# Last block of a two-block network: where the delta rule's key products, first inverses, solve and chunks stand in the hand-written order

## The chip, the cores and the metric

The kernel runs on one core of one Trainium2 chip. The metric is the time of one execution on the device, in microseconds (us), as the median of several runs. A core has a matrix engine (TensorE, PE in the profile; its weight loads are PEld), a vector engine (DVE), an activation engine (ACT), GpSimd (POOL) and a queue that issues the large loads (SP). Each engine runs its own program in order and waits for the others on counters.

## What is computed

The reference is a network of two parts on 512 tokens of width 1024. The first part is two layers with four mixers and a mixture of 16 experts. The second part, the last block, is what the change touches. Cut to what matters here:

```python
def second_block(x, ...):
    h = rmsnorm(x, ln1[l]);  proj = h @ w_in[l]
    qkv_a, z_a, b_a, a_a, q_b, k_b, v_b = jnp.split(proj, IN_SPLITS, axis=-1)
    y_a = gated_deltanet(qkv_a, z_a, b_a, a_a, ...)      # 4 heads of 128
    y_b = dilated_attention(q_b, k_b, v_b, slopes)       # 8 heads of 64
    x = x + concatenate([y_a, y_b]) @ w_out[l]
    ...                                                  # then a gated FFN of width 2816

def chunk_gated_delta_rule(q, k, v, g, beta):            # within gated_deltanet
    decay = exp(where(causal, g_i - g_j, -inf))
    a = where(strict, (k * beta) @ k.T * decay, 0)       # per chunk
    u, w = solve((I + a), [v * beta, k * beta * exp(g)])
    a_qk = where(causal, q @ k.T * decay, 0)
    for each chunk:                                      # a recurrence over the state
        v_new = u - w @ state
        o = (q * exp(g)) @ state + a_qk @ v_new
        state = state * exp(g_last) + (k * exp(g_last - g)).T @ v_new
    y = o * rsqrt(mean(o*o)) * norm_gain * silu(z)
```

The kernel uses chunks of 128 tokens, so there are four, t = 0 to 3, and four heads, h = 0 to 3.

## The kernel before, in words

All engines of the last block walk one list, `second_plan()` (lines 488 to 545), and each emits what an entry means for it, in the order of the list. So an entry that is moved in the list is moved on every engine at once, and whatever follows it on an engine waits behind it. The list has three stretches.

**The projection stretch** has 16 pieces, k = 0 to 15: the q and k columns of the attention, then its values (8 to 11), then z, the gate input (12 to 15, two rows of weight blocks each, 24 matmuls over 512 columns). Between the pieces stand the norms, the turning of keys and values to token order, the decays (`decay`, k = 10 to 13, one head each: TensorE spreads the summed log-decay over the partitions at line 1307, DVE subtracts at lines 2564 and 2566, ACT takes the exponentials at lines 1837 and 1839 into `WS[h]` and `CMS[h]`) and GpSimd's scaling of keys (`keys`, `kdec`). Weights are split into a high and a low part on ACT (line 1464) and on DVE or GpSimd (lines 1989, 2748), two steps ahead.

**The attention stretch** has 37 items, k = 0 to 36. Item k holds a pipelined step of the dilated attention (`attend`): TensorE's scores of item k (line 1245), the transposes of item k-2 (line 842), the values of item k-3 (line 1259); DVE adds the bias to the scores of k-1 (line 2514), takes maxima (2517, 2519), the reciprocal of k-2 (2523) and scales the output of k-3 (2530); ACT takes Exp of k-1 (line 1783) and copies. The 32 score tiles go through `heads2`, four query tiles for each of 8 heads; a tile has 128, 256, 384 or 512 columns. Between them stand the delta rule's entries:

- `head` h, items 0 to 3: TensorE forms k k' (called kk) and q k' (kq) at line 1316 and spreads beta (bb) at line 1313. DVE makes, in order, kk times the decays (line 2573), times beta (2576), masks it to the first level (2578), forms the first inverse `UU[h]` = I minus it (2580), copies the last decay of each chunk (2581), and makes the query side: kq times the decays (2584) and q times exp(g) (2585). GpSimd's part is the causal mask on the decays `WS[h]` (line 2864). It comes after DVE's line 2573, and DVE's line 2584 waits for it.
- `first` (transposing `UU[h]`) and `mask` 1: items 1 to 4. The solve doubles the inverted blocks in six levels per head, 24 steps: `cm` (line 1332, copied by ACT at 1855, mask for the next level by GpSimd at 2872) from item 4, `onward` (lines 1339 and 1344, added by DVE at 2590 and 2594) from item 5, `nw` (line 1352) in items 26 to 29.
- The chunks: `vnew` t (lines 1364, 1366, copied by ACT at 1865), `out` t (lines 1376, 1382, 1383; DVE updates the state at 2607 or 2610; ACT squares the output at 1871; DVE sums at 2614, 2616), `gate` t (ACT takes a Sqrt at 1876; DVE lines 2622, 2624, 2627, 2631 follow) and `flip` t (transposes, line 842). The earliest item of each stands in `starts`: `vnew` 0 in item 30, `gate` 0 in item 32.

**The mix stretch** follows: `y2` entries split the attention's and the delta rule's outputs (ACT line 1889, DVE line 2635), `early` splits the first weights of the output projection, and `mix` multiplies (lines 1227 to 1229). The last chunks stand between them.

TensorE's accumulators are 8 banks. Those of the projections and of the attention (`flow`) turn in a ring of four, those of the delta rule (`rule`) in another ring of four. A bank is taken again only when its last content has been read. In a plain item the attention takes three banks, so the transposes of item k take the bank that held the scores of item k-1, which DVE's line 2514 frees.

## Time and profile before

| | us |
|---|---|
| median of 3 runs | 2709.71 |
| lowest and highest | 2708.41, 2711.92 |
| profiled execution, its own time | 2714.45 |
| its span, first to last instruction | 2712.4 |
| stretch of z's last two pieces on TensorE | 2079.8 to 2091.2 |
| attention stretch and last chunks, to the fourth tile of the first mix | 2091.2 to 2286.3 |

The last two lines are read from the order of TensorE's instructions in the trace: first instruction of line 1245 at 2091.20, and the matmuls of lines 1227 to 1229 that follow the last transposes, at 2286.28. Times in the trace are counted from the start of the span. TensorE's clock stands in it as a share of full speed: 1.00 is 2.4 GHz, 0.50 is 1.2 GHz, and the mean over a stretch tells how much of it ran at either level. "Busy" of PE means that a matmul was in flight; idle is what is left. In brackets behind an instruction stands how long its engine had been idle before it and what it waited for.

### The profile page before, as it was taken

Reading aid. Unit: us, or ns where it says so; the run is one execution under the profiler, and the core shown is the slowest. Engines: PE = TensorE matmul, PEld = TensorE weight load, DVE = VectorE, ACT = ScalarE, POOL = GpSimd, SP = SyncE. Lnnn points to the kernel's source line nnn. Section 1 sums busy time; section 2 is a strip of 40 time slices with the busy share of each in tenths; the row PEclk is TensorE's granted clock in tenths of the full one; section 3 lists DMA queues with packets and bytes.
Section 4 is the critical chain, followed back from the end, with each engine's and each line's share of the span. In section 5 each row is a group of like instructions: output and inputs, shape, how many; then the busy total and the mean of one; then the engine's idle time right before and its main releaser. Section 6 shows DMA issues by size and latency. Waiting matters only on the chain.

```text
span 2712.4 us, 35451 instructions
## 1 busy us (share of the span) xinstructions
PE 2523.3 (93%) x13952; PEld 1538.8 (57%) x13952; DVE 1291.1 (48%) x2479; ACT 1002.6 (37%) x1871; POOL 403.3 (15%) x276
## 2 busy tenths in 40 slices
PE   6998997899999997997969999998999898999998
PEld 4875566433333332775744334442767787788886
DVE  3596435344444444676452333334664555442342
ACT  5226542334444444536523222223343233322222
POOL 0223002001111101223100000001124211222221
PEclk9999999899999998998989999999999898999999
DMA  6216734689999996220039999998120002222221
GB/s 274 67 47 230 271 153 178 247 333 378 380 393 387 386 396 241 98 78 1 32 141 422 421 421 421 420 421 331 59 82 20 12 19 106 87 94 93 93 86 55
DMA packets 85467, 567.71 MB, mean 209 GB/s; under 512 B 11760, under 2 KB 12016, under 8 KB 20280
## 3 DMA queue, kind: packets, MB, share of 16 engines
q1 hardware_dynamic: 79944, 550.15, 51.7%
q0 software_dynamic: 3616, 11.80, 2.0%
q10 hardware_dynamic: 1744, 3.51, 0.4%
q8 instruction: 112, 1.84, 0.3%
q14 instruction: 51, 0.42, 0.0%
HBM read 550.74 MB, written 14.68 MB: 208 GB/s over the span
## 4 chain that ended last, share of the span: by engine, by line
PE 75%; DVE 5%; ACT 3%; DMA 1%; issue 1%; DVEq 0%; SPq 0%; ACTq 0%
PE PS L1098 24%; PE PS L1104 6%; PE PS L1213 4%; PE PS L1215 4%; PE PS L1214 4%; PE PS L1227 4%; PE PS L1229 4%; PE PS L1228 4%; PE PS L1172 3%; PE PS L1203 2%; PE PS L842 2%; DMA RF<-in_w_down_dram 1%; PE PS L1339 1%; PE PS L1034 1%; PE PS L924 1%
## 5 line engine op out<-in xcount | busy, mean ns | idle before, releaser
L2748 POOL TENSOR_TENSOR WHL<-RING,WHL 128x1024 fp32r<-128x1024 f32 x64 | 172.2, 2691 | 1361.5 <-ACT WHL L1464 1361.5
L1464 ACT ACTIVATE WHL<-RING 128x1024 fp32r<-128x1024 f32 x129 | 134.6, 1047 | 206.9 <-PE PS L1229 129.4
L1213 PE MATMUL PS<-RR,WHL 128*128 128x512 f32 x512 | 205.1, 401 | 1.8 <-DVE RR L2501 1.8
L1215 PE MATMUL PS<-RR,WHL 128*128 128x512 f32 x512 | 202.6, 396 | 0.0
L1214 PE MATMUL PS<-RR,WHL 128*128 128x512 f32 x512 | 202.0, 395 | 0.0
L1098 PE MATMUL PS<-RING,RF 128*64 128x512 f32 x816 | 185.3, 598 | 0.7 <-issue 0.7
L1098 PE MATMUL PS<-WIDE,RF 128*64 128x512 f32 x792 | 182.0, 596 | 0.0
L1989 DVE TENSOR_TENSOR WHL<-RING,WHL 128x1024 fp32r<-128x1024 f32 x65 | 81.7, 1259 | 165.8 <-ACT WHL L1464 159.6
L1734 ACT ACTIVATE RF<-PS,MODS,MSC 128x128 f32<-128x128 f32 x192 | 73.2, 445 | 182.8 <-PE PS L1172 129.9
L1098 PE MATMUL PS<-RF 128*64 128x512 f32 x544 | 127.5, 596 | 0.5 <-DMA RF<-in_w_down_dram 0.5
L1098 PE MATMUL PS<-X,RF 128*64 128x512 f32 x528 | 123.4, 598 | 0.5 <-DMA X<-in_w_down_dram 0.5
L1098 PEld LDWEIGHTS PS<-RING,RF 128*64 128x64 f32 x816 | 55.9, 137 | 112.1 <-issue 105.4
L1098 PEld LDWEIGHTS PS<-WIDE,RF 128*64 128x64 f32 x792 | 53.8, 137 | 112.9 <-issue 108.3
L1229 PE MATMUL PS<-WHL,AS 128*128 128x512 f32 x288 | 114.4, 397 | 0.0
L2073 DVE SCALAR_TENSOR_TENSOR AR<-AR,VEC 128x497 f32<-128x497 f32 (+29 forms) x180 | 111.8, 693 | 0.0
L1213 PEld LDWEIGHTS PS<-RR,WHL 128*128 128x128 f32 x512 | 96.1, 188 | 26.7 <-issue 2.8
L2430 DVE TENSOR_TENSOR RF<-PS,RF 64x512 f32<-64x512 f32 x64 | 43.5, 680 | 142.3 <-ACT RF L1715 142.2
L1214 PEld LDWEIGHTS PS<-RR,WHL 128*128 128x128 f32 x512 | 96.1, 188 | 24.9 <-issue 1.7
L1215 PEld LDWEIGHTS PS<-RR,WHL 128*128 128x128 f32 x512 | 96.1, 188 | 23.3
L2403 DVE TENSOR_TENSOR RF<-PS,RF 64x512 f32<-64x512 f32 x64 | 43.6, 681 | 117.3 <-ACT RF L1680 117.3
L1227 PE MATMUL PS<-WHL,AS 128*128 128x512 f32 x248 | 99.0, 399 | 0.0
L1228 PE MATMUL PS<-WHL,AS 128*128 128x512 f32 x248 | 98.5, 397 | 0.0
(405 smaller groups left out, 5168.1 us busy)
## 6 DMA issues: line engine op xcount, KB each, us to landing
RING<-in_w_gate_dram SPq DMA_DIRECT2D x60, 1024.0 KB, 8.5
WIDE<-in_w_down_dram SPq DMA_DIRECT2D x52, 1024.0 KB, 11.3
RING<-in_ada_w_dram SPq DMA_DIRECT2D x48, 1024.0 KB, 5.8
RING<-in_w_up_dram SPq DMA_DIRECT2D x44, 1024.0 KB, 8.8
X<-in_w_gate_dram SPq DMA_DIRECT2D x39, 1024.0 KB, 8.4
AR<-in_w_up_dram SPq DMA_DIRECT2D x37, 1024.0 KB, 9.6
RF<-in_w_down_dram SPq DMA_DIRECT2D x31, 1024.0 KB, 13.7
RING<-in_w_in_dram SPq DMA_DIRECT2D x30, 1024.0 KB, 5.2
```

The source lines that it names most:

```text
L1098: ins = e.matmul(a[r:r + 64, :], xs[:, j, 0:64], w[:, i, :], start=begin and i < 2, stop=end and i > 1)
L1104: ins = e.matmul(b[r:r + 32, :], xs[:, j, 64:96], w[:, i, :], start=begin, stop=end)
L1213: e.matmul(o, h[:, j, :], HTH2[:, j, :], start=j == 0, stop=False)
L1214: e.matmul(o, h[:, j, :], HTL2[:, j, :], start=False, stop=False)
L1215: ins = e.matmul(o, lo[:, j, :], HTH2[:, j, :], start=False, stop=j == 7)
L1227: e.matmul(o, hi(j)[:, z], h[:, i, :], start=j == 0, stop=False)
L1228: e.matmul(o, hi(j)[:, z], lo[:, i, :], start=False, stop=False)
L1229: ins = e.matmul(o, lo_(j)[:, z], h[:, i, :], start=False, stop=j == k - 1)
L1464: e.activation(h, load_buffer(ld)[:, js, cs], ACT.Copy).then_inc(act, A(("hi", st["i"])))
L1989: e.tensor_tensor(lo, load_buffer(loads[st["load"]])[:, js, cs], h.bitcast(F32), ALU.subtract).then_inc(dve, V(("lo", st["i"])))
L2073: e.scalar_tensor_tensor(y, UB[:, i, t0 + lo + d:t0 + hi + d], VEC[:, w:w + 1], y, ALU.mult, ALU.add).then_inc(dve, V(*([("conv", l, s)] i ...
L2748: e.tensor_tensor(lo, load_buffer(loads[st["load"]])[:, js, cs], h.bitcast(F32), ALU.subtract).then_inc(pool, G(("lo", st["i"])))
```

## The change

In the list of the last block:

- `head` now holds only the key side: kk and bb on TensorE, and DVE's lines 2573 to 2580. It stands in the projection stretch, head 0 behind z's second piece (k = 13), heads 1 and 2 behind the third and the fourth, head 3 behind them all.
- The causal mask is an entry of its own, `causal` h, at k = 11 to 14. It waits for ACT's exponential of the decays, and DVE's line 2573 now waits for it, so kk is multiplied by masked decays. The first-level mask keeps a part of the causal half, so the result is the same.
- The copy of the last decays is an entry `last`, four of them at k = 13, in front of head 0.
- The query side is an entry `query` h, in items 0 to 3 (kq on TensorE, DVE's lines 2584 and 2585), together with `first` h and `mask` 1.
- `cm` starts in item 2 instead of 4, `onward` in item 3 instead of 5, `nw` in item 24 instead of 26.
- The chunks start in item 28 instead of 30, and `vnew` 2, `gate` 1, `out` 2, `flip` 1 and `vnew` 3 get items 33 to 36. Before, `vnew` 2 stood in item 35, `gate` 1 in item 36, and `out` 2, `flip` 1 and `vnew` 3 behind the items; in the mix stretch `gate` 2 now stands in front of the `y2` entries.

No instruction is added or taken away, and no load or other DMA is moved in the list; the load that waits for the last `onward` is issued when that is done.

```diff
--- before.py
+++ after.py
@@ -509,38 +509,39 @@
             plan.append(("eg",))
         if 10 <= k <= 13:
             plan += [("decay", k - 10), ("keys", k - 10)]
+        if 11 <= k <= 14:
+            plan.append(("causal", k - 11))
+        if k == 13:
+            plan += [("last", h) for h in range(4)] + [("head", 0)]
         if k == 14:
             plan.append(("kdc",))
         if k >= 14:
-            plan += [("kdec", 2 * (k - 14)), ("kdec", 2 * (k - 14) + 1)]
-    plan.append(("zsilu",))
+            plan += [("kdec", 2 * (k - 14)), ("kdec", 2 * (k - 14) + 1), ("head", k - 13)]
+    plan += [("head", 3), ("zsilu",)]
 
     wy = [(s, h) for s in range(1, 7) for h in range(4)]
     chunks = [("vnew", 0), ("out", 0), ("vnew", 1), ("gate", 0), ("out", 1), ("flip", 0), ("vnew", 2), ("gate", 1),
               ("out", 2), ("flip", 1), ("vnew", 3), ("gate", 2), ("out", 3), ("flip", 2), ("gate", 3), ("flip", 3)]
-    starts = {("vnew", 0): 30, ("out", 0): 31, ("vnew", 1): 32, ("gate", 0): 32, ("out", 1): 33, ("flip", 0): 34}
+    starts = {("vnew", 0): 28, ("out", 0): 29, ("vnew", 1): 30, ("gate", 0): 30, ("out", 1): 31, ("flip", 0): 32,
+              ("vnew", 2): 33, ("gate", 1): 34, ("out", 2): 35, ("flip", 1): 36, ("vnew", 3): 36}
     for k in range(37):
         if k < 36:
             plan.append(("attend", k))
         if k < 4:
-            plan.append(("head", k))
-        if 1 <= k <= 4:
-            plan += [("first", k - 1), ("mask", 1, k - 1)]
-        if 0 <= k - 5 < 24:
-            plan.append(("onward", *wy[k - 5]))
-        if 0 <= k - 4 < 24:
-            n, h = wy[k - 4]
+            plan += [("query", k), ("first", k), ("mask", 1, k)]
+        if 0 <= k - 3 < 24:
+            plan.append(("onward", *wy[k - 3]))
+        if 0 <= k - 2 < 24:
+            n, h = wy[k - 2]
             plan.append(("cm", n, h))
             if n < 6:
                 plan.append(("mask", n + 1, h))
-        if 26 <= k < 30:
-            plan.append(("nw", k - 26))
-        while chunks and k >= starts.get(chunks[0], 35 if chunks[0][0] != "flip" else 36):
+        if 24 <= k < 28:
+            plan.append(("nw", k - 24))
+        while chunks and k >= starts.get(chunks[0], 37):
             plan.append(chunks.pop(0))
-            if chunks and chunks[0] not in starts:
-                break
-    assert chunks[0] == ("out", 2)
-    plan += [("out", 2), ("flip", 1), ("y2", 4), ("y2", 5), ("y2", 6), ("y2", 7), ("vnew", 3), ("gate", 2), ("early",),
+    assert chunks[0] == ("gate", 2)
+    plan += [("gate", 2), ("y2", 4), ("y2", 5), ("y2", 6), ("y2", 7), ("early",),
              ("out", 3), ("flip", 2), ("mix", 0, 0), ("gate", 3), ("mix", 0, 1), ("mix", 0, 2), ("flip", 3), ("mix", 0, 3)]
     return plan + [("mix", 2, t) for t in range(4)] + [("y2", j) for j in range(4)]
 
@@ -1307,14 +1308,18 @@
                         e.matmul(o, HSEL[:, 128 * h:128 * h + 128], GR, start=True, stop=True).then_inc(pe, P(("gb", h)))
                     elif what == "head":
                         h, = k
-                        for name, f, free in (("kk", 4 + h, "kkd"), ("bb", 0, "at"), ("kq", h, "aq")):
-                            o = bank(rule, (name, h), (V, (free, h)))
-                            if name == "bb":
-                                ins = e.matmul(o, HSEL[:, 128 * h:128 * h + 128], BR, start=True, stop=True)
-                            else:
-                                for z in tiles4:
-                                    ins = e.matmul(o[:, z], C[:, 4 + h, z], C[:, f, z], start=True, stop=True)
-                            ins.then_inc(pe, P((name, h)))
+                        o = bank(rule, ("kk", h), (V, ("kkd", h)))
+                        for z in tiles4:
+                            ins = e.matmul(o[:, z], C[:, 4 + h, z], C[:, 4 + h, z], start=True, stop=True)
+                        ins.then_inc(pe, P(("kk", h)))
+                        o = bank(rule, ("bb", h), (V, ("at", h)))
+                        e.matmul(o, HSEL[:, 128 * h:128 * h + 128], BR, start=True, stop=True).then_inc(pe, P(("bb", h)))
+                    elif what == "query":
+                        h, = k
+                        o = bank(rule, ("kq", h), (V, ("aq", h)))
+                        for z in tiles4:
+                            ins = e.matmul(o[:, z], C[:, 4 + h, z], C[:, h, z], start=True, stop=True)
+                        ins.then_inc(pe, P(("kq", h)))
                     elif what == "first":
                         h, = k
                         o = bank(rule, ("u0T", h), (A, ("u0T", h)))
@@ -2569,7 +2574,7 @@
                         h, = k
                         u3 = UU[:, h, :].rearrange("p (t i) -> p t i", i=128)
                         e.wait_ge(pe, P["kk", h])
-                        e.wait_ge(act, A["egb", h])
+                        e.wait_ge(pool, G["causal", h])
                         e.tensor_tensor(AT[:, h, :], held("kk", h), WS[h], ALU.mult).then_inc(dve, V(("kkd", h)))
                         e.wait_ge(dve, V.n)
                         e.wait_ge(pe, P["bb", h])
@@ -2578,9 +2583,13 @@
                         e.tensor_tensor(u3, AT[:, h, :].rearrange("p (t i) -> p t i", i=128), m0, ALU.mult).then_inc(dve, V())
                         e.wait_ge(dve, V.n)
                         e.scalar_tensor_tensor(u3, u3, -1.0, idb, ALU.mult, ALU.add).then_inc(dve, V(("u0", h)))
+                    elif what == "last":
+                        h, = k
+                        e.wait_ge(act, A["egb", h])
                         e.tensor_copy(DL[:, h, :], CMS[h].rearrange("p (t i) -> p t i", i=128)[:, :, 127]).then_inc(dve, V())
+                    elif what == "query":
+                        h, = k
                         e.wait_ge(pe, P["kq", h])
-                        e.wait_ge(pool, G["causal", h])
                         e.tensor_tensor(AQ[:, h, :], held("kq", h), WS[h], ALU.mult).then_inc(dve, V(("aq", h)))
                         e.tensor_tensor(C[:, h, :], C[:, h, :], CMS[h], ALU.mult).then_inc(dve, V(("qdec", h)))
                     elif what == "onward":
@@ -2857,10 +2866,10 @@
                     t, = k
                     e.wait_ge(act, A["kdc",])
                     e.tensor_tensor(KTOK[:, t, :, :], KTOK[:, t, :, :], by_token(KDC, t), ALU.mult).then_inc(pool, G(("kdec", t)))
-                elif what == "head":
+                elif what == "causal":
                     h, = k
                     d3 = WS[h].rearrange("p (t i) -> p t i", i=128)
-                    e.wait_ge(dve, V["kkd", h])
+                    e.wait_ge(act, A["dec", h])
                     e.tensor_tensor(d3, d3, cau, ALU.mult).then_inc(pool, G(("causal", h)))
                 elif what == "mask":
                     n, h = k
```

## Rows read from the trace of the kernel before

**Rows 1.** Busy time of TensorE over the whole span (part 1 of the page).

```profile
PE 2523.3 (93%) x13952; PEld 1538.8 (57%) x13952; DVE 1291.1 (48%) x2479; ACT 1002.6 (37%) x1871; POOL 403.3 (15%) x276
```

**Rows 2.** Windows: length, busy time (instructions) of PE, PEld, DVE, ACT, POOL; PE clock, DMA.

```profile
2139.86:2224.06 84.20, 79.72 (x607) 69.18 (x606) 48.26 (x127) 29.52 (x74) 21.64 (x17) 1.00 0.06 17
...
2224.06:2286.28 62.22, 52.04 (x332) 45.52 (x331) 35.83 (x82) 26.02 (x54) 5.22 (x2) 0.86 0.24 89
2245.90:2252.20 6.30, 4.41 (x25) 4.26 (x24) 2.65 (x7) 1.80 (x5) 0.00 (x0) 0.73 0.25 99
2256.80:2269.20 12.40, 9.41 (x45) 8.94 (x46) 4.71 (x12) 1.89 (x4) 0.00 (x0) 0.59 0.01 1
2275.90:2283.00 7.10, 4.23 (x15) 3.37 (x14) 6.86 (x5) 2.75 (x4) 5.08 (x2) 0.76 0.00 0
2117.85:2139.86 22.01, 21.09 (x123) 18.21 (x122) 9.98 (x28) 6.89 (x17) 5.08 (x4) 0.74 0.04 13
2091.20:2117.85 26.65, 21.36 (x99) 14.14 (x98) 21.21 (x39) 8.67 (x17) 9.64 (x7) 0.83 0.04 10
```

**Rows 3.** Timeline of TensorE, items 0 to 4: start, duration, line, count, idle.

```profile
2091.62 1.16 PE L1316 MATMUL PS<-AR 128*128 128x128 f32 x8
2092.71 1.12 PE L1313 MATMUL PS<-VECY,ROUTER 4*128 4x512 f32 x2
...
2103.02 1.16 PE L1316 MATMUL PS<-AR 128*128 128x128 f32 x8 [0.77 <-DVE RF L2584]
...
2110.56 0.69 PE L1259 MATMUL PS<-AR,WIDE 128*128 128x64 f32 x2 [4.52 <-DVE WIDE L2514]
...
2119.56 0.90 PE L842 MATMUL PS<-CON,WIDE 128*128 128x128 f32 x3 [0.92 <-DVE WIDE L2514]
```

**Rows 4.** DVE from 2091.2 to 2121, grouped by line: count, busy us, mean ns, idle.

```profile
L2580 DVE SCALAR_TENSOR_TENSOR RF<-RF,CON 128x512 f32<-128x512 f32 x4 | 4.7, 1164 | 0.1
L2578 DVE TENSOR_TENSOR RF<-RF,CON 128x512 f32<-128x512 f32 x4 | 4.0, 1008 | 0.1
...
L2573 DVE TENSOR_TENSOR RF<-PS,X 128x512 f32<-128x512 f32 x4 | 2.7, 686 | 12.9 <-PE PS L1316 12.9
L2584 DVE TENSOR_TENSOR RF<-PS,X 128x512 f32<-128x512 f32 x4 | 2.7, 680 | 0.0
```

**Rows 5.** Timeline of DVE at the first key product.

```profile
2092.82 0.69 DVE L2573 TENSOR_TENSOR RF<-PS,X 128x512 f32<-128x512 f32 x1 [11.55 <-PE PS L1316]
```

**Rows 6.** Timeline of TensorE: one solve step, items 23 and 24.

```profile
2212.67 1.11 PE L1339 MATMUL PS<-RF,X 128*128 128x128 f32 x8
2213.62 1.06 PE L1344 MATMUL PS<-X,RF 128*128 128x128 f32 x8
2214.51 1.06 PE L1332 MATMUL PS<-RF,ROW 128*128 128x128 f32 x8
2215.50 0.48 PE L1245 MATMUL PS<-RF 64*128 64x128 f32 x2
```

**Rows 7.** Timeline of ACT and DVE around the first gate (item 32).

```profile
2246.40 0.69 DVE L2614 TENSOR_REDUCE SM<-RF 128x4 f32<-128x512 f32 x1 [0.64 <-ACT RF L1871]
...
2252.05 0.60 ACT L1865 ACTIVATE RF<-PS 128x512 f32<-128x512 f32 x1 [2.03 <-PE PS L1366]
...
2252.66 1.28 ACT L1876 ACT_TABLE_LOAD   x1
...
2253.96 0.20 ACT L1876 ACTIVATE SM<-SM 128x4 f32<-128x4 f32 x1
...
2255.93 0.69 DVE L2631 TENSOR_TENSOR RF<-RF,AR 128x512 f32<-128x512 f32 x1
```

**Rows 8.** Timeline of TensorE: waits of the last chunks, items 32 to 36 and mix.

```profile
2247.94 0.66 PE L1259 MATMUL PS<-AR,WIDE 128*128 128x64 f32 x4 [1.89 <-DVE WIDE L2514]
...
2259.65 1.08 PE L842 MATMUL PS<-CON,WIDE 128*128 128x128 f32 x4 [2.25 <-DVE WIDE L2530]
...
2278.90 0.71 PE L842 MATMUL PS<-CON,RF 128*128 128x128 f32 x4 [2.87 <-DVE RF L2631]
```

## The prediction

> **What bounds the kernel now.** I read the page's busy times first: TensorE is in flight for 93% of the span [rows 1], so a change in order can give back only TensorE's idle time and the time its clock is low. Next come the windows over the attention stretch [rows 2]. Items 0 to 3 take 26.65 us with 5.3 idle, at a mean clock of 0.83; items 4 to 7 take 22.01 with 0.9 idle, at 0.74. A mean clock c over L us means 2(1-c)L at the low level, so 9.1 and 11.4 us: one low stretch of 20.5 us. Items 8 to 25 take 84.20 us at full clock with 4.5 idle, 4.68 us an item. From item 26 to the fourth tile of the first mix it is 62.22 us with 10.2 idle and a clock of 0.86, 17.4 us low. The rest of the span is not touched.
>
> Then the timelines, to see who is waited for. In items 0 to 4 TensorE waits three times, each time for DVE [rows 3]: 0.77 us for the query product, 4.52 and 0.92 us for the bias addition that frees the scores' bank. There DVE does seven delta-rule operations an item beside the attention: 2573, 2576, 2584 and 2585 at 0.69 us, 2578 and 2580 at 1.0 and 1.16 us on average [rows 4], as they run against GpSimd's masks, and a short copy; about 5.2 us in items that give TensorE 3.7 to 5.5 us of work. Before that DVE stood idle for 11.55 us beside z's last pieces [rows 5]. At the other end the waits of 1.89, 2.25 and 2.87 us [rows 8] are all for DVE, each with a low stretch: 3.4 us (6.30 at 0.73), 10.2 us (12.40 at 0.59), 3.4 us (7.10 at 0.76) [rows 2].
>
> **The change, part by part.**
>
> *Key products moved.* kk and bb occupy TensorE for 1.09 and about 1.05 us start to start, and 1.12 less the overlap [rows 3], so 4 x 2.14 = 8.6 us move from the items into the projection stretch. TensorE is full there, so this gives nothing by itself. Two more changes between the two kinds of matmul come with it; no row here prices one, I take 0.2 us each; bounds 0 and the 0.77 of the nearest wait. The attention then starts at 2091.2 + 8.6 + 0.4 = 2100.2.
>
> *DVE's half of a head* (2573 to 2580) is 0.69 + 0.69 + 1.01 + 1.16 = 3.5 us at the rows' means, 2.8 us without GpSimd beside it. Heads 0 and 1 lie in the 11.55 us that DVE was idle. Head 2's kk ends at about 2097 and head 3's bb at 2100.2; the two chains in a row (4 x 0.69 us each and gaps) end near 2103. The masks and key scalings of GpSimd (4 x 1.27 and 4 x 1.0 us) have the same gap. ACT's last z copy, four Silu and two table loads (1.28 us each as in [rows 7]), about 5 us behind z's end near 2096, end near 2101, before the first transposes are there to copy. If DVE were full, each 1 us of delay would show at item 0.
>
> *Items 0 to 3.* The full-clock work of items 0 to 3 now is 21.4 less half of the low time in which it was busy (9.1 less some 2 idle), 17.8. Take off 8.6, add what comes two items earlier: one `onward`, two `cm` and a `first` (1.84 + 2 x 0.99 + 0.53, [rows 6]; the last from an item's difference) = 4.4: 13.6 us. DVE has only 1.4 us of query work an item. The first bias addition waits behind head 3 and query 0, near 2104.5; the first exponential ends at 2105.7, when TensorE has been ready for 0.6 us. So item 4 starts at 2100.2 + 13.6 + 0.6 = 2114.4, against 2117.85: the waits of 6.2 us shrink to 0.6. Bounds of that wait: 0 and 6.2. What is late next is again the bias addition, by 0.7 us in every fourth item, as now.
>
> *Items 4 to 7* then run like items 8 to 25: 4 x 4.68 = 18.7 against 22.01 at mixed clock. Item 8 starts at 2133.1. Items 8 to 25 keep their contents but for the last three, which lose two of line 1344's products and gain two `nw`, 0.2 us more, and one 0.7 us wait goes: 83.7. Item 26 starts at 2216.8 instead of 2224.06. That is 7.3 us, and the solve is two items further: two `onward`, two `cm`, two `nw` = 5.9 us of TensorE work less to do behind it.
>
> *Item 26 to the mix.* Full-clock work now: 52.0 busy less half the low busy time (17.4 less 1.7) = 44.2; after: 38.3. Here the change adds a wait. `gate` 0 moves to item 30, with two attention tiles to come. DVE waits there for ACT's Sqrt, which stands behind the copy of `vnew` 1 and a table load, and behind it on DVE is the bias addition that frees the bank for item 31's transposes. The rows of the same gate [rows 7]: copy at 2252.05, load, Sqrt at 2253.96, last DVE operation ends at 2256.62: 4.6 us from the copy. Add 0.6 for a bias addition and 0.1 to start: item 31 is held for 5.3 us, of which its scores cover 1.05. New wait: 4.3 us. In the same manner `out` 0 in item 29 puts a sum [rows 7] and a short operation before item 30's bias addition: 1.4 us. `out` 1 does so before item 32: 1.8 us (1.89 at the same place now, [rows 8]). Then 0.5 for the bank that `gate` 1 frees, 0.2 for the state, 0.8 for ACT's copy of `vnew` 3, 0.8 for `gate` 2, 2.8 before the mix (`gate` 2 now stands before the y2 work, four times 0.63 us on DVE, and the first weights' split of 2.4 us on GpSimd ends late too), 2.0 for `gate` 3 through DVE's slow split: together 14.6 us of waits, against 10.2. These follow from the order and the durations in rows; bounds 8 and 18.
>
> *The clock.* Behind the wait of 4.5 us the clock was low for 20.5 us; behind 1.9, 2.25 and 2.9 us for 3.4, 10.2 and 3.4. A 4.3 us wait is nearest to the first; I take 16 us low for the whole tail, 2.6 of it idle, so 6.7 us lost; bounds 3.4 and 40. Tail: 38.3 + 14.6 + 6.7 = 59.6 us instead of 62.2. With 3.4 us low it is 54.
>
> *Sum.* 2216.8 + 59.6 = 2276.4 against 2286.28: **9.9 us less**. After that the mix and the FFN are full on TensorE. The profiled execution took 2714.45 us, its span 2712.4; they become 2704.6 and 2702.5. Taken from the median of 2709.71 it is 2699.8, so **2700 us**.
>
> A rule that speaks against the change. In the trace, the first gate's Sqrt starts 0.02 us after its table load of 1.28 us [rows 7], and Exp of the last tile is done by then. After the change Exp is needed twice more behind that Sqrt, so ACT loads two tables more: one back to Exp, beside DVE's gate, and one before `gate` 1, which I have counted in the 0.5 us. The Trainium skill, page "ScalarE: Activation LUTs", section "Table sets: the hidden batching unit", says to do all Exp and then all Sqrt, and prices a switch in "What ACT_TABLE_LOAD costs" at 2.66 us, 1.38 of it a drain behind the load. By that figure two switches wholly on the path would be 5.3 us and the time 2705; the row shows no drain there.
>
> **The rivals.**
>
> *The tail takes more back.* The low clock of item 31 holds through the sparse items 32 to 35 up to the mix (40 us low, 5 idle: 17.5 lost instead of 6.7, but some waits are covered by the slower work, I take 5 us net), or both added loads delay DVE (1.28 + 1.28 us). For it: those items are half empty and TensorE waits again in each. Against: low stretches here ended in 3.4 and 10.2 us. Time: 2705.
>
> *The head keeps its low stretch.* The waits go, but the clock falls anyway at the change from z to items 0 to 2, which carry little work. Then half of 20.5 less the 2 us idle in it, 9 us, stays: 2709. Against: items 8 to 25 have 4.5 us idle in short pieces and stay at full clock [rows 2].
>
> *Slower.* A wait of over 2 us behind head 3 starts a low stretch in item 0 or 1, and it does not end soon. Each us of busy time at the low level costs half a us, so from 20 us on the gain is used up; one of 35 us (items 1 to 5) costs 17: 2717. For it: the present one lasted 20.5 us though TensorE was busy for nearly all of it behind the wait (items 4 to 7 have 0.9 us idle, [rows 2]). Against: it ended by itself in item 6, with the same contents.
>
> *It does not do what it says.* Heads in the projection stretch could hold up z. Only if a bank of kk waits for DVE's 2573 two heads before, which ended 6 us earlier: no price.
>
> *Better.* The added wait leaves the clock full for nearly all the tail, 54 us: 2694.
>
> **How the numbers follow.** The forecast 0.61 (2697 to 2703), the tail takes more 0.14 (2705), better 0.08 (2694), the head keeps its low stretch 0.09 (2709), slower 0.08 (2717). The range leaves out the slower case, the head's, and little of the better one: 2693.5 to 2708. Faster by over 0.2% (5.4 us, about what a measurement of this kernel can tell from no change, so below 2704.3) is the forecast, the better case and about half of the tail's: 0.75. Within 0.2%: the rest of the tail's and most of the head's, 0.16. Slower by more: 0.09.
>
> **What the profile after would show.** Right: DVE's line 2573 starts near 2083 rather than 2092.8, four times; line 1245's first instruction near 2100; no wait over 1 us in items 0 to 4 and clock 1.00 in 2100 to 2215; item 26 near 2217; a wait of about 4 us before item 31's line 842, put down to line 2514, with DVE's 2622 waiting for ACT's Sqrt ahead of it; three table loads behind item 29 instead of one; the fourth mix tile near 2276. Wrong: a low clock near 2105, z's matmuls stretched beyond 11.3 us plus the moved work, or item 31 without a wait, which would mean that I read the ring of banks wrongly.

## The result, and the profile after

| | before | after |
|---|---|---|
| median, us | 2710.95 (19 runs) | 2717.45 (19 runs) |
| lowest and highest | 2706.04, 2715.41 | 2712.20, 2720.01 |
| profiled execution, its span | 2714.45, 2712.4 | 2720.01, 2717.9 |
| first `gb` product to item 26, in the trace | 165.92 | 157.06 |
| item 26 to the fourth tile of the first mix | 62.22 | 72.11 |
| from there to the end | 426.12 | 426.05 |

The kernel became 0.24% slower: ratio 1.0024, 95% interval 1.0017 to 1.0031. The forecast was 2700 us with a range of 2693.5 to 2708; the measured time lies outside it, on the other side of the kernel before.

The distances are counted from the first product that spreads the decays (line 1307 before, 1308 after), because what lies ahead of it varies by up to 5 us between executions of the same code (it stood at 2058.14 before and at 2062.68 after), and the change does not touch it. I call the way from there to the fourth tile of the first mix "the stretch": 228.14 us before, 229.17 after. The two traces differ in it by 1.0 us only, the medians by 6.5. The two profiled executions as wholes differ by 5.6 us, and 4.5 of them lie ahead of the first `gb` product; what the trace of before has to do with the rest comes out at the end of the experiments.

The page's busy times, which answer [rows 1], are the same work but for two more instructions on ACT. These are the two table loads that the forecast counted (40 in the trace instead of 38, and three behind item 29 instead of one):

```profile
PE 2523.4 (93%) x13952; PEld 1538.5 (57%) x13952; DVE 1287.4 (47%) x2479; ACT 1004.4 (37%) x1873; POOL 404.4 (15%) x276
```

The windows of after, which answer [rows 2] (columns as there): items 0 to 25; item 26 to the fourth mix tile; and three parts of the latter.

```profile
2104.11:2219.74 115.63, 110.52 (x834) 95.25 (x833) 70.29 (x182) 43.27 (x107) 30.50 (x24) 1.00 0.06 15
2219.74:2291.85 72.11, 50.40 (x284) 43.27 (x283) 32.52 (x77) 26.11 (x52) 5.66 (x2) 0.81 0.20 77
2229.60:2239.00 9.40, 4.22 (x20) 4.22 (x21) 1.17 (x6) 1.09 (x3) 0.00 (x0) 0.64 0.58 240
2250.00:2269.00 19.00, 15.70 (x82) 14.99 (x83) 5.69 (x19) 6.08 (x13) 0.00 (x0) 0.66 0.00 0
2278.00:2291.85 13.85, 7.98 (x29) 6.13 (x27) 9.81 (x12) 4.24 (x7) 5.66 (x2) 0.75 0.22 76
```

The first row is the half that went as planned: all 26 items at full clock. The second is where the gain went. 21.7 us without a matmul in flight instead of 10.2, and a mean clock of 0.81, which over 72.11 us is 27.4 us at the low level instead of 17.4. The third row holds the oddest part: 9.4 us with 4.2 busy, while the DMA engines move 240 GB/s.

The clock was at the low level four times in this stretch. The sum of the windows 2232.30:2239.12, 2249.36:2256.19, 2259.60:2266.43 and 2283.50:2290.32, which have it at 0.50 throughout:

```profile
sum 27.30, PE 22.82 PEld 21.21 DVE 10.43 ACT 6.04 POOL 4.37; mean PE 5.70 PEld 5.30 DVE 2.61 ACT 1.51 POOL 1.09
```

TensorE was in flight for 22.8 us of them. So the 72.1 us are 21.7 of waits, 11.4 lost to the clock (half of the 22.8) and 39.0 of work at full clock.

TensorE's timeline at the head, which answers [rows 3]. There are two waits in items 0 to 5 instead of three, and the 4.52 us are gone:

```profile
2104.11 0.48 PE L1246 MATMUL PS<-RF 64*128 64x128 f32 x2
...
2109.65 0.30 PE L843 MATMUL PS<-CON,WIDE 128*128 128x128 f32 x1 [0.54 <-ACT WIDE L1788]
...
2117.76 0.48 PE L1246 MATMUL PS<-RF 64*128 64x128 f32 x2
2118.91 0.55 PE L843 MATMUL PS<-CON,WIDE 128*128 128x128 f32 x3 [0.67 <-DVE WIDE L2519]
```

And its waits in the tail, which answer [rows 8]:

```profile
2234.78 1.11 PE L843 MATMUL PS<-CON,WIDE 128*128 128x128 f32 x4 [5.20 <-DVE WIDE L2519]
...
2241.89 0.33 PE L843 MATMUL PS<-CON,WIDE 128*128 128x128 f32 x1 [1.11 <-DVE WIDE L2519]
...
2250.04 0.69 PE L843 MATMUL PS<-CON,WIDE 128*128 128x128 f32 x2 [4.08 <-DVE WIDE L2519]
...
2259.20 0.78 PE L1260 MATMUL PS<-AR,WIDE 128*128 128x64 f32 x4 [2.57 <-DVE WIDE L2519]
...
2284.61 0.80 PE L1228 MATMUL PS<-WHL,RR 128*128 128x512 f32 x1 [5.34 <-POOL WHL L2757]
```

Three of them need a second look, since each names only the last engine in a row of waits.

**The 5.20 us.** DVE's bias addition (line 2519) was late because it stood itself, for a DMA. Timeline of DVE:

```profile
2234.43 0.29 DVE L2519 TENSOR_TENSOR WIDE<-PS,AR 128x128 f32<-128x128 f32 x1 [6.10 <-DMA AR<-in_bias_dram]
```

Timelines of SyncE's and ACT's queues, the issues of that time:

```profile
2222.72 0.33 SPq L810 DMA_DIRECT2D X<-in_w_out_dram  x1
2223.14 1.61 SPq L810 DMA_DIRECT2D RING<-in_w_out_dram  x3
```

```profile
2226.56 0.33 ACTq L1781 DMA_DIRECT2D AR<-in_bias_dram  x1
```

The DMA view from 2212 to 2250 (KB of each, median us to landing):

```profile
RING<-in_w_out_dram SPq DMA_DIRECT2D x3, 1024.0 KB, 7.2
...
AR<-in_bias_dram ACTq DMA_DIRECT2D x1, 256.0 KB, 7.8
```

The four loads of the output projection, 1 MB each, wait on SyncE's queue for the solve's last product. The solve ends two items sooner, so they are issued 3.8 us ahead of the last head's bias load, which ACT issues in its own item as before. The bias lands 7.8 us after its issue, at 2234.4, when the four megabytes are nearly through. In the kernel before, the same bias load was issued 2.2 us ahead of those loads, and it landed in 2.7 us. Timelines of its two queues, and its DMA view from 2226 to 2260:

```profile
2233.55 0.33 ACTq L1776 DMA_DIRECT2D AR<-in_bias_dram  x1
2235.78 0.33 SPq L809 DMA_DIRECT2D X<-in_w_out_dram  x1
...
AR<-in_bias_dram ACTq DMA_DIRECT2D x1, 256.0 KB, 2.7
```

**The 4.08 us** is gate 0, as the forecast had it. Timeline of ACT around it, which answers [rows 7]:

```profile
2244.95 0.60 ACT L1870 ACTIVATE RF<-PS 128x512 f32<-128x512 f32 x1 [1.67 <-PE PS L1371]
2245.56 1.28 ACT L1881 ACT_TABLE_LOAD   x1
2246.86 0.20 ACT L1881 ACTIVATE SM<-SM 128x4 f32<-128x4 f32 x1
2247.08 1.28 ACT L1788 ACT_TABLE_LOAD   x1
...
2250.79 0.61 ACT L1788 ACTIVATE WIDE<-WIDE,SM 128x384 f32<-128x384 f32 x1 [2.43 <-DVE SM L2524]
```

DVE stands for it, with the bias addition of item 31 behind the gate's operations (timeline of DVE):

```profile
2247.09 0.18 DVE L2631 RECIPROCAL SM<-SM 128x4 f32<-128x4 f32 x1 [3.70 <-ACT SM L1881]
...
2249.43 0.55 DVE L2519 TENSOR_TENSOR WIDE<-PS,AR 128x384 f32<-128x384 f32 x1
```

The second table load, back to Exp, costs nothing here: it ends at 2248.36, and ACT then waits 2.43 us for DVE.

**The 5.34 us** names GpSimd's split of the first output weights, whose own wait names ACT. ACT's split in turn (timeline of ACT) waited for DVE's `y2` operations:

```profile
2281.08 2.00 ACT L1469 ACTIVATE WHL<-X 128x1024 fp32r<-128x1024 f32 x2 [2.96 <-DVE RR L2644]
```

and those stand on DVE behind gate 2 in the new order (timeline of DVE):

```profile
2278.42 2.49 DVE L2644 TENSOR_TENSOR RR<-WIDE,RR 128x512 fp32r<-128x512 f32 x4
```

So ACT's split starts at 2281.1, GpSimd's at 2282.2, and TensorE gets its weights at 2284.6.

### The profile page after: what moved, and what is told of

Its sections match the earlier page's. It is cut to its first block, busy times and chain, and to the rows that moved or that the text cites. A ratio compares the mean times of both kernels' runs of the same rounds, so it can differ in the third digit from the quotient of the medians.

```text
span 2717.9 us, 35449 instructions
## 1 busy us (share of the span) xinstructions
PE 2523.4 (93%) x13952; PEld 1538.5 (57%) x13952; DVE 1287.4 (47%) x2479; ACT 1004.4 (37%) x1873; POOL 404.4 (15%) x276
## 4 chain that ended last, share of the span: by engine, by line
PE 75%; DVE 4%; ACT 3%; DMA 2%; issue 1%; POOL 0%; SPq 0%; ACTq 0%; DVEq 0%
PE PS L1099 24%; PE PS L1105 6%; PE PS L1214 4%; PE PS L1216 4%; PE PS L1215 4%; PE PS L1228 4%; PE PS L1230 4%; PE PS L1229 4%; PE PS L1173 3%; PE PS L1204 2%; PE PS L843 2%; DMA RF<-in_w_down_dram 1%; PE PS L1035 1%; PE PS L1344 1%; PE PS L925 1%
## 5 line engine op out<-in xcount | busy, mean ns | idle before, releaser
L2757 POOL TENSOR_TENSOR WHL<-RING,WHL 128x1024 fp32r<-128x1024 f32 x64 | 172.5, 2696 | 1363.4 <-ACT WHL L1469 1363.4
## 6 DMA issues: line engine op xcount, KB each, us to landing
RF<-in_w_down_dram SPq DMA_DIRECT2D x31, 1024.0 KB, 13.7
```

The source lines that it names most:

```text
L2757: e.tensor_tensor(lo, load_buffer(loads[st["load"]])[:, js, cs], h.bitcast(F32), ALU.subtract).then_inc(pool, G(("lo", st["i"])))
```

## The experiments

Each ratio below compares runs with runs of the kernel before on the same chip. The experiments were run on several chips, on which the kernel before had medians from 2709.0 to 2711.3 us, so a difference between the medians of two experiments is good to some 2 us; where it matters I give it by the ratios too. "Stretch" is read from the one trace of each, and line numbers shift by a few.

**The bias load first.** In the changed kernel SyncE waits until the last bias load has landed before it issues the output projection's loads; ACT issues the bias load where it did.

```diff
                 if "scratch" in ld:
+                    e.wait_ge(bias_in[1], 16 * 4)
                     e.wait_ge(pe, P["du", 6, 3])
```

> The changed kernel, with one wait added on the load queue: the output projection's four loads of 1 MB are not issued before the attention's last bias tile (256 KB) has landed. Theory C (collision): in the changed kernel the last solve step is done 13 us sooner, so these loads start at 2222.7 us, ahead of the last bias load (issued at 2226.56), which then takes 7.8 us to land instead of 2.7; the bias addition waits 6.10 us for it, TensorE 5.20 us, and a low clock follows. Then the wait of 5.20 us in item 29 goes, and the stretch from item 26 to the fourth mix tile shrinks from 72.2 us by 5.2 and by the low clock behind it (9.4 us at 0.64, some 2.5 us lost), to 64.5 us, and the median from 2717.5 to about 2710. Rival G (the gate is the bound): the wait for the first gate in item 31, 4.08 us, and its bank just take over what is freed, and the stretch stays over 69 us, the median over 2715.

Measured: 2710.68 us (12 runs), ratio 1.0001 (0.9991 to 1.0010), stretch 222.77 us, nearly as theory C had it. In the timelines the bias load is issued at 2221.54 and the loads at 2224.03, and the wait of 5.20 us is gone. The window from item 26 to the fourth mix tile:

```profile
2214.72:2280.43 65.71, 49.73 (x283) 42.47 (x283) 32.50 (x77) 26.00 (x52) 5.66 (x2) 0.82 0.22 85
```

One added wait on an idle queue gives back 6.8 us by the medians (6.2 by the ratios) and 6.4 in the trace. That settles the collision as the largest single cause. Counted from item 26 the loads start 6.3 us later than in the changed kernel (9.31 against 2.98), and nothing waits for them.

**Gate 0 behind the last exponentials.** `gate` 0 goes from item 30 to item 32, `flip` 0 to 34.

```diff
-    chunks = [("vnew", 0), ("out", 0), ("vnew", 1), ("gate", 0), ("out", 1), ("flip", 0), ("vnew", 2), ("gate", 1),
+    chunks = [("vnew", 0), ("out", 0), ("vnew", 1), ("out", 1), ("gate", 0), ("vnew", 2), ("flip", 0), ("gate", 1),
...
-    starts = {("vnew", 0): 28, ("out", 0): 29, ("vnew", 1): 30, ("gate", 0): 30, ("out", 1): 31, ("flip", 0): 32,
+    starts = {("vnew", 0): 28, ("out", 0): 29, ("vnew", 1): 30, ("gate", 0): 32, ("out", 1): 31, ("flip", 0): 34,
```

> The changed kernel, with the first gate moved from item 30 to item 32, behind the last Exp of the attention, the first flip to item 34 and the third new-value product in front of it. Theory G: the wait of 4.08 us in item 31 and the 1.11 to 2.57 us around it come from the gate standing ahead of a bias addition on the vector engine. Then no wait over 2 us is left in items 30 to 32 and one table load of the activation engine goes; the stretch from item 26 to the fourth mix tile shrinks by 4 to 7 us (with the low clock behind it), the median to 2711 to 2713. Theory C alone (only the bias load matters): the work moved meets the same wait later, and the stretch shrinks by less than 2 us.

Measured: 2712.40 us (12 runs), ratio 1.0011 (1.0001 to 1.0020), stretch 224.29 us. The wait of 4.08 us is gone, the one for the bias is still there (4.44 us). The window from item 26 to the fourth mix tile:

```profile
2218.18:2285.42 67.24, 49.83 (x284) 42.60 (x283) 32.41 (x77) 23.49 (x50) 5.67 (x2) 0.80 0.22 83
```

It gives back 5 us by the medians and in the trace (3.5 by the ratios), within what was expected. The edit moves the whole gate with all that it waits for, so it does not price the table switch by itself.

**The y2 entries sooner.** `y2` 4 to 7 stand at the end of item 35, in front of `flip` 1, instead of behind `gate` 2.

```diff
+        if k == 35:
+            plan += [("y2", 4), ("y2", 5), ("y2", 6), ("y2", 7)]
...
-    plan += [("gate", 2), ("y2", 4), ("y2", 5), ("y2", 6), ("y2", 7), ("early",),
+    plan += [("gate", 2), ("early",),
```

> The changed kernel, with the split of the attention's output (four y2 entries) moved from behind the third gate to the end of item 35. Theory Y: the wait of 5.34 us before the first mix matmul is not the weights as such; the activation engine may split them only behind the last of these y2 entries, which now stand behind the third gate on the vector engine. Then the wait falls below 1.5 us and the stretch from item 26 to the fourth mix tile shrinks by 4 to 5 us, the median to about 2713. Rival: the wait for the fourth gate and flip, which the present wait covers, takes its place, and less than 2 us is gained.

Measured: 2715.10 us (12 runs), ratio 1.0017 (1.0009 to 1.0026), stretch 226.25 us. TensorE's timeline before the mix:

```profile
2276.96 0.63 PE L845 MATMUL PS<-CON,RF 128*128 128x128 f32 x4 [2.87 <-DVE RF L2642]
...
2283.97 0.63 PE L845 MATMUL PS<-CON 128*128 128x128 f32 x4 [2.18 <-DVE CON L2642]
```

The wait of 5.34 us is replaced by 2.87 in front of `flip` 2 and 2.18 in front of `flip` 3. The weights come in time, and now the gates' own chains are last. It gives back 2.4 us by the medians (1.9 by the ratios) and 2.9 in the trace. That is less than the 4 to 5 us of theory Y and more than the rival's 2: most of the old wait only hid those of the gates.

**The keys alone.** The kernel before with `head`, `causal`, `last` and `query` as the change has them (`first` and `mask` 1 one item sooner with them), and with the solve, the chunks and the mix where they were.

```diff
+        if 11 <= k <= 14:
+            plan.append(("causal", k - 11))
+        if k == 13:
+            plan += [("last", h) for h in range(4)] + [("head", 0)]
...
+            plan += [("kdec", 2 * (k - 14)), ("kdec", 2 * (k - 14) + 1), ("head", k - 13)]
+    plan += [("head", 3), ("zsilu",)]
...
-            plan.append(("head", k))
-        if 1 <= k <= 4:
-            plan += [("first", k - 1), ("mask", 1, k - 1)]
+            plan += [("query", k), ("first", k), ("mask", 1, k)]
```

> Only the first half of the change: the key side of the heads and the causal mask stand in the projection stretch as in the changed kernel, the query side in items 0 to 3; the solve, the chunks and the mix stand where they stood before. The head's part of the prediction: waits of 6.2 us shrink to 0.6 and the low clock of 20.5 us goes. The changed kernel's trace had this at 8.9 us less to item 26 with 5.9 us more work done, so 14 us should be gained here, with the tail as before: 62 us from item 26 to the fourth mix tile, median 2696 to 2698. Rival: a part of the low clock or of the waits only moves into the longer plain items, and less than 8 us is gained.

Measured: 2700.81 us (6 runs), ratio 0.9966 (0.9954 to 0.9978), stretch 211.37 us. Windows of items 0 to 25 and of item 26 to the fourth mix tile:

```profile
2102.69:2214.49 111.80, 105.42 (x785) 89.83 (x784) 68.04 (x177) 40.92 (x103) 30.53 (x24) 1.00 0.05 15
2214.49:2272.63 58.14, 47.93 (x331) 41.54 (x331) 35.81 (x82) 26.02 (x54) 5.21 (x2) 0.94 0.26 96
```

So the first half of the change makes the kernel some 10 us faster, and the second half takes 16.6 us back (2717.45 less 2700.81; 15.7 by the ratios). The expected 2696 to 2698 us were missed by 3 us, though in the trace the stretch fell by 16.8 us, more than the 14 expected; why both is answered at the end of the experiments. Here the bias load is issued at 2224.00 and the output loads at 2226.21, as far apart as before.

**Gate 0 behind out 1, in the kernel with the keys alone.**

```diff
-    chunks = [("vnew", 0), ("out", 0), ("vnew", 1), ("gate", 0), ("out", 1), ("flip", 0), ("vnew", 2), ("gate", 1),
+    chunks = [("vnew", 0), ("out", 0), ("vnew", 1), ("out", 1), ("gate", 0), ("vnew", 2), ("flip", 0), ("gate", 1),
...
-    starts = {("vnew", 0): 30, ("out", 0): 31, ("vnew", 1): 32, ("gate", 0): 32, ("out", 1): 33, ("flip", 0): 34}
+    starts = {("vnew", 0): 30, ("out", 0): 31, ("vnew", 1): 32, ("out", 1): 33, ("gate", 0): 33,
+              ("vnew", 2): 34, ("flip", 0): 35}
```

> The keys alone with gate 0 behind out 1 (item 33 instead of 32), vnew 2 an item sooner (34) and flip 0 an item later (35). In the run of the keys alone, the waits of TensorE in the tail are 1.89, 2.25, 0.73, 0.96, 0.78, 2.87 and 0.60 us. Theory A (what gate 0 costs is its table switch in front of an item's exponentials, as the 4.9 us that moving it brought in the changed kernel): the 1.89 us wait goes and little comes for it, stretch 208 to 210.5 us, time 2698 to 2700 us. Theory B (the wait only moves to the next place where VectorE or ScalarE is late): stretch within 1 us of 211.4, time 2700 to 2702 us. If flip 0 an item later makes a new wait in front of item 35's work, the stretch is over 212.5 us.

Measured: 2701.06 us (9 runs), ratio 0.9967 (0.9957 to 0.9978), stretch 211.43 us: no difference, and my theory A was wrong. The wait of 1.89 us is still there:

```profile
2239.79 0.66 PE L1262 MATMUL PS<-AR,WIDE 128*128 128x64 f32 x4 [1.89 <-DVE WIDE L2521]
```

In item 32 gate 0 already stands behind the last exponential. So in these runs it cost something where exponentials were still to come, as behind the move to item 30, and nothing here. What sets the 1.89 us instead was not tested.

**All three mends.** The changed kernel with the three edits above at once.

> The changed kernel with the three edits of e2, e3 and e4 at once: the last bias load ahead of the output projection's loads, the first gate behind the last exponentials, y2 4 to 7 sooner. Theory A (three separate waits, each of which holds the end of the stretch): the savings add, 6.4 + 4.9 + 2.9 = 14.2 us, so that the stretch from the first gb product to the fourth mix tile takes 229.2 - 14.2 = 215.0 us (range 212 to 218) and the time is near 2717.5 - 14.2 = 2703.3 us (2700 to 2707), ratio .997. It then still stands some 3 us behind the keys alone (211.4 us, 2700.8 us), and the pure shift of the solve and chunks brings nothing. Theory B (the waits hide one another: once one goes, the next holds the same end): the sum falls short, stretch above 218 us, time above 2707 us. Theory C (the three hid a real gain of the shift): stretch under 211 us, time under 2700 us.

Measured: 2702.22 us (9 runs), ratio 0.9971 (0.9956 to 0.9987), stretch 213.33 us, where item 0 stands 1.5 us later than in the other traces of kernels with the keys' half. That is a spell of low clock ahead of item 0, in z's last pieces, while TensorE was in flight all the time. The windows of that place, and of item 26 to the fourth mix tile:

```profile
2060.00:2082.00 22.00, 22.00 (x87) 14.88 (x86) 7.46 (x33) 9.07 (x15) 11.68 (x10) 1.00 0.00 0
2082.00:2086.00 4.00, 4.00 (x11) 3.14 (x12) 3.51 (x5) 0.46 (x2) 4.00 (x4) 0.57 0.02 4
2216.69:2271.42 54.73, 42.23 (x283) 35.79 (x283) 33.85 (x77) 23.50 (x50) 5.23 (x2) 0.94 0.27 101
```

The single savings were 6.8, 5.0 and 2.4 us by the medians, 14.2 together; all at once they bring 15.2. By the ratios it is 11.7 and 14.4, in the traces 14.2 and 15.8. So within the noise they add, and they account for nearly all of the 16.6 us. With them the shift of solve and chunks is free, but it brings nothing: this kernel is not ahead of the keys alone.

**Keys and solve, chunks as before.** The keys' half, `cm`, `onward` and `nw` two items sooner, the chunks at their old items.

```diff
-        if 0 <= k - 5 < 24:
-            plan.append(("onward", *wy[k - 5]))
-        if 0 <= k - 4 < 24:
-            n, h = wy[k - 4]
+        if 0 <= k - 3 < 24:
+            plan.append(("onward", *wy[k - 3]))
+        if 0 <= k - 2 < 24:
+            n, h = wy[k - 2]
...
-        if 26 <= k < 30:
-            plan.append(("nw", k - 26))
+        if 24 <= k < 28:
+            plan.append(("nw", k - 24))
```

> The keys' half (as the run of the keys alone, 211.4 us from the first gb product to the fourth mix tile, 2700.8 us) and the solve two items sooner, but the chunks at the items where the kernel before has them. Theory A (moving the solve's end ahead of the bias load makes the collision, whatever the chunks do): item 26 stands at +157 us from the first gb product, the output projection's loads are issued ahead of the last bias load, VectorE waits 4 to 6 us for the bias, and the stretch takes 211.4 + 5 to 7 = 217 to 219 us; time 2706 to 2709 us. Gate 0's wait stays near 1.9 us, as in the kernel before. Theory B (the chunks' shift is what brings the waits): no wait for the bias over 1 us, stretch 210 to 213 us, time 2699 to 2703 us.

Measured: 2710.65 us (10 runs), ratio 1.0002 (0.9991 to 1.0013), stretch 221.42 us, 2.4 us above the top of the expected range; the wait is as expected. Timeline of DVE, and the window from item 26 on:

```profile
2230.66 0.29 DVE L2520 TENSOR_TENSOR WIDE<-PS,AR 128x128 f32<-128x128 f32 x1 [5.41 <-DMA AR<-in_bias_dram]
```

```profile
2216.65:2280.99 64.34, 48.51 (x284) 40.61 (x283) 33.74 (x77) 23.76 (x50) 5.23 (x2) 0.84 0.23 85
```

The solve's shift alone, with no chunk moved, turns the gain of the keys into nothing. The 10 us it costs are about twice the wait of 5.45 us on TensorE. Much of the rest is clock: 0.84 over 64.34 us is 20.6 us at the low level, against 7.0 us for the keys alone.

**The same with the bias load first.** The same kernel with the wait on SyncE of the first experiment.

> The keys' half and the solve two items sooner, chunks where the kernel before has them, and SyncE's wait that keeps the output projection's loads behind the last bias load. Without that wait this kernel measured 221.4 us from the first gb product to the fourth mix tile (2710.65 us), with a wait of 5.45 us for the bias; the keys alone measured 211.4 us (2700.8 us). Theory A (all of the 10 us between them is the collision: the wait and the low clock behind it): the 5.45 us wait is gone, the granted clock of the tail is back near .94, stretch 210.5 to 213 us, time 2700 to 2703 us. Theory B (the earlier solve costs by itself, for instance since items 26 to 35 have less other work between their steps, and the pipeline's waits show): stretch 214 us or more, new waits in items 28 to 31 that sum to 2 us or more, time above 2703 us.

Measured: 2700.72 us (10 runs, 2693.39 to 2708.12), ratio 0.9963 (0.9950 to 0.9977), stretch 215.62 us, with the same 1.5 us ahead of item 0. Windows of that place, and of item 26 to the fourth mix tile:

```profile
2082.00:2086.00 4.00, 4.00 (x11) 2.77 (x10) 2.97 (x5) 1.09 (x3) 3.42 (x4) 0.59 0.02 4
2217.31:2274.33 57.02, 45.80 (x284) 39.42 (x283) 33.71 (x77) 23.53 (x50) 5.21 (x2) 0.88 0.26 97
```

The median is that of the keys alone, so by the medians all 10 us of the kernel above are the collision, as theory A has it, though these runs spread widely and the interval leaves 3.6 us on either side. The traces show less: the stretch fell by 5.8 us, or 7.3 without the 1.5, and missed theory A's 210.5 to 213 us. The clock of 0.88 instead of 0.94 is 13.7 us at the low level instead of 7.0. Theory B's new waits of 2 us did not come: the only new one is 1.09 us. So most of the 10 us is shown to be the collision; whether 3 us of it are something else is open.

**Chunks one item sooner.** The kernel above, with keys, solve and bias load first, and other `starts`. `vnew` 0, `out` 0, `vnew` 1, `out` 1 and `vnew` 2 go one item sooner, `gate` 0 and `flip` 0 one item later, which made no difference by itself in the kernel with the keys alone.

```diff
-    chunks = [("vnew", 0), ("out", 0), ("vnew", 1), ("gate", 0), ("out", 1), ("flip", 0), ("vnew", 2), ("gate", 1),
+    chunks = [("vnew", 0), ("out", 0), ("vnew", 1), ("out", 1), ("gate", 0), ("vnew", 2), ("flip", 0), ("gate", 1),
...
-    starts = {("vnew", 0): 30, ("out", 0): 31, ("vnew", 1): 32, ("gate", 0): 32, ("out", 1): 33, ("flip", 0): 34}
+    starts = {("vnew", 0): 29, ("out", 0): 30, ("vnew", 1): 31, ("out", 1): 32, ("gate", 0): 33,
+              ("vnew", 2): 34, ("flip", 0): 35}
```

> As the kernel above (keys, solve two items sooner, bias load first) with the chunks' first steps one item sooner: vnew 0 at item 29, out 0 30, vnew 1 31, out 1 32, gate 0 33, vnew 2 34, flip 0 35. Theory A (TensorE's busy time is the floor here, and only the drain behind item 31 and the gates' chains stay): what work moves ahead of the drain no longer fills it, so the sum of waits stays within 1 us of the kernel above, stretch 210.5 to 213 us, time 2700 to 2703 us. Rival (one item is the right distance: the solve leaves room that the chunks can fill, without the gates' steps standing in front of exponentials): stretch under 209.5 us, time under 2699 us.

Measured: 2698.23 us (8 runs), ratio 0.9959 (0.9947 to 0.9971), stretch 207.97 us.

```profile
2218.41:2269.33 50.92, 41.30 (x283) 34.85 (x283) 33.76 (x77) 23.32 (x50) 5.22 (x2) 0.97 0.29 109
```

This is the fastest kernel of the study, some 12 us ahead of the kernel before and 19 ahead of the changed one. By the trace the rival's 209.5 us is undercut: TensorE is idle behind item 26 for 9.6 us instead of 11.2, and only 3.1 us run at the low clock. By the medians it is 2.5 us ahead of the same kernel without the shift of one item, and the two intervals overlap, so that the last step helps is likely, not shown.

**The changed kernel again**, for a second trace:

> The changed kernel, unchanged, for a second profiled execution. The first took 229.2 us from the first gb product to the fourth mix tile, with a wait of 5.20 us for the last bias load and a granted clock of .81 behind item 26. If the collision is in every run of it: a wait of 4 to 6 us for the bias load, stretch 227 to 230 us. If it is a matter of chance: no wait for the bias over 2 us, stretch near 222.8 us, as with the bias load put first.

Measured: 2720.29 us, stretch 229.68 us. Timeline of DVE:

```profile
2233.45 0.29 DVE L2519 TENSOR_TENSOR WIDE<-PS,AR 128x128 f32<-128x128 f32 x1 [5.36 <-DMA AR<-in_bias_dram]
```

The collision is no accident of one execution.

**The kernel before again, twice.** The traces of before and of the keys alone differ by 16.8 us in the stretch, the medians by 10. Of this gap of some 7 us, 3.1 lie ahead of the first `gb` product (2058.14 and 2061.26), and 3.8 are what the profiled execution of before took above its median. Of the 5.5 us between the stretches (1.0) and the medians (6.5) of before and after, 4.5 lie ahead. Both gaps leave a part that points to the trace of before.

> The kernel before, unchanged, for a second profiled execution. Its first one took 2714.45 us, some 3.5 us above the median of its runs, with 228.1 us from the first gb product to the fourth mix tile; the keys alone took 211.4 us there, 16.8 us less, but by the medians they gain 9 to 10 us only. Theory A (the length of low clock behind the waits at the attention's start differs from run to run of the kernel before, and its first profile caught a long one): this execution shows the same waits, but a stretch of 218 to 226 us, and less time at the low clock between 2091 and 2112 us than 20.5 us. Theory B (the stretch is the same in every run and what differs is elsewhere): 227.5 to 229 us again.

> The kernel before once more, unchanged. Its two profiled executions took 2714.45 and 2715.61 us at a mean granted clock of .967, both with 228.2 us from the first gb product to the fourth mix tile; over its 68 runs the time follows the mean clock, 2714.5 us at .967, 2709.1 at .970 and 2705.7 at .972. If this execution has .967 again, the stretch is 228 us again and nothing new is learned. If it has .969 or more, theory A (the spells at the low clock inside the stretch differ in length between runs) expects a stretch of 227 us or less, with the same waits; theory B (the clock differs elsewhere in the program) expects 228.2 us and fewer microseconds outside it.

Measured: 2715.61 us and a stretch of 228.19 us in the second trace, which spoke for theory B; then 2705.93 us and 219.32 us in the third, which decides for theory A. The third was taken on another chip, but another execution on that same chip took 2715.93 us at a mean clock of 0.967, so it is not the chip. Windows of the third: items 0 to 25, item 26 to the fourth mix tile, and 25 us around the first waits.

```profile
2091.54:2219.93 128.39, 117.67 (x826) 97.47 (x825) 79.50 (x192) 44.87 (x108) 36.40 (x28) 0.96 0.06 15
2219.93:2277.79 57.86, 48.92 (x332) 42.60 (x331) 35.82 (x82) 26.02 (x54) 5.21 (x2) 0.91 0.26 96
2110.00:2135.00 25.00, 23.18 (x141) 18.78 (x142) 14.48 (x38) 7.65 (x20) 7.59 (x6) 0.82 0.05 11
```

The last window in the first trace of before:

```profile
2110.00:2135.00 25.00, 23.52 (x113) 19.59 (x113) 11.50 (x31) 6.29 (x16) 6.30 (x5) 0.62 0.03 11
```

TensorE waits at the same places for the same times (0.78, 4.52, 0.92; 1.89, 1.71 for 2.25, 2.87), but the low clock behind them is much shorter: about 10.3 us instead of 20.5 in items 0 to 25, 10.4 instead of 17.4 behind item 26. That is most of the 8.8 us by which the same program's stretch differs. Over the 69 runs of the kernel before that were made beside these experiments, the time goes with the mean granted clock (levels with one run left out):

| mean clock of the run | runs | median, us |
|---|---|---|
| 0.967 | 7 | 2714.5 |
| 0.968 | 6 | 2712.4 |
| 0.969 | 19 | 2712.4 |
| 0.970 | 21 | 2709.2 |
| 0.971 | 9 | 2707.0 |
| 0.972 | 5 | 2705.7 |

The trace on which the forecast rests had 0.967, at the slow end of this table.

## Why the prediction was wrong

By its own steps, in order:

*Key products moved: right.* Item 0 starts 8.4 us later from the first `gb` product (41.43 us against 33.06); forecast 9.0.

*DVE's half of a head, items 0 to 3: right.* Items 0 to 3 take 13.65 us and hold one wait, of 0.54 us; forecast 13.6 + 0.6. The low clock at the head is gone, in every kernel with this half.

*Items 4 to 25: right.* Items 0 to 25 take 115.6 us; the forecast's 2100.2 to 2216.8 is 116.6. To item 26 the change gained 8.9 us in the trace, forecast 7.3. Part of that is the execution: against the third trace of before, with its shorter low spell, it is 4.4 us (161.46 us from the first `gb` product to item 26, against 157.06).

*Item 26 to the mix: wrong.* The sum was 38.3 of work, 14.6 of waits and 6.7 of clock, 59.6; measured were 39.0, 21.7 and 11.4, 72.1. The waits named there were mostly right: 1.4 in item 30 (1.11), 4.3 for gate 0 (4.08), 1.8 behind `out` 1 (2.57), 0.5, 0.2, 0.8 and 0.8 of the chunks (0.47, 0.31, 0.97, 0.78). The 2.0 us for gate 3 do not show; the wait before the mix covers them, and with `y2` moved 2.18 us appear in front of `flip` 3. Three things went wrong.

First, **a step is missing**. The change moves the last `onward`, and the text priced it on TensorE, DVE, ACT and GpSimd, but not on SyncE, whose queue waits for it. The chapter on the change even says that the load that waits for the last `onward` is issued when that is done. That moves 4 MB forward by 17.6 us, counted from the first `gb` product (177.64 to 160.04; 13 us by the positions in the two traces), past a load that somebody is waiting for. The forecast had nothing for it. The wait is 5.20 us; with the clock behind it the cost is 6.8 us by the medians in the changed kernel, and 10 us in the kernel where keys and solve are moved (5.8 us in the traces). None of the rivals held it.

Second, **the wait before the mix was mis-sized**: 2.8 us forecast, 5.34 measured. The text placed gate 2 in front of the `y2` work and saw GpSimd's split late, but it did not follow ACT's splits back to their own wait for `y2` 7. The experiment that moves `y2` gives 2.4 us back. It also shows why not more: 2.87 us of DVE's chain in front of `flip` 2 come back, as in the kernel before [rows 8].

Third, **the clock was mis-sized**: 16 us low forecast, 27.4 measured, within its bounds of 3.4 and 40. With the bias load first it is still 0.82 over 65.7 us, 23.7 us low, so most of this excess does not come from the missing step. The third trace of before shows that the wait alone does not fix this quantity. Behind the same 4.52 us the clock was low for 20.5 us in one execution and 10.3 in another.

*The sum and its baseline: wrong.* The 9.9 us were worked out from a trace with a stretch of 228.1 us and then taken from the median of other runs. Those runs have, by their mean clock, less low time to lose: by the medians the keys' half gained 10 us, where the stretch in the first trace shows 16.8 and against the third 8.0. So even a right price list would probably have come out too fast by some microseconds, since the low clock of that trace was one of its gains; that is worked out from the three traces and the mean clocks, not tested.

*The rival "slower"* put the danger at the head, behind head 3. It had the right sign and the wrong place, so its 2717 us, which is the measured time, is luck. Its "against" also misread the low spell of before: by the clock in the trace it ran from 2108.6 to 2129.1 and ended in item 5 and not in item 6. "The tail takes more back" had the right place, but a price of 5 us above the forecast, where the tail took 12.5 us more.

On gate 0 the rows and the experiment say: moved behind the last Exp it gives back 5.0 us. The Sqrt starts 1.30 us after the start of its table load, and DVE stands for 3.70 us, in which ACT also makes the copy of `vnew` 1. The Trainium skill, page "ScalarE: Activation LUTs", section "Table sets: the hidden batching unit", has the rule to do all Exp and then all Sqrt; it speaks against the new order, and the experiment agrees in sign, without pricing the switch alone. The same page's section "What ACT_TABLE_LOAD costs" has 2.66 us for a switch. The trace does not show that: the 1.30 us are all there is between the start of the load and the Sqrt, and the load back to Exp is hidden.

For the collision: the traces have a 256 KB load that takes 2.7 us when it is issued ahead of four 1 MB loads and 7.8 us behind them, though another engine had issued those. The Trainium skill, page "DMA: Bandwidth & Descriptors", section "Issuing engines are not separate DMA queues", says that transfers started by different engines run on the same 16 DMA engines and interleave. The traces agree in so far as a queue of its own did not protect this small load.

The account by medians: 2710.7 us before (69 runs); the keys' half −9.9, to 2700.8; the solve two items sooner +9.8, to 2710.65, and the same kernel with the bias load first returns to 2700.7; the chunks two items sooner +6.8, to 2717.45, of the size of the 5.0 and 2.4 us measured for gate 0 and `y2`. These medians come from several chips, so each step is good to some 2 us. What stays open: what decides how long the clock stays low behind a wait, why it fell in two traces behind no wait at all, and whether the earlier solve costs up to 3 us beside the collision.

## What to carry to other kernels

When a step is moved, list what waits for it on every queue, those that only issue loads above all. A load that becomes free to go sooner is not a gain unless somebody waits for it, and it can pass in front of a small load that somebody does wait for; let the large ones wait for the small one. Before a gain that consists of low clock is taken from a median, compare the mean clock of the profiled execution with that of the median run.
